# The last attention and the closing rows of a two-block transformer kernel: another order of work, and a value product in two reduced-precision passes

## The chip, the cores and the metric

The kernel runs on one core of a Trainium2 chip. Its inputs and output are fp32 arrays in HBM. The metric is the device time of one execution in microseconds, the median of several. TensorE multiplies matrices into PSUM (eight banks of 128 x 512 fp32), VectorE and ScalarE work on elements, GpSimd does elementwise work in SBUF only, and SyncE issues the DMAs. The engines run their own lists of instructions in order and meet at semaphores.

## The reference

512 tokens of width 1024 go through a first block (sparse attention, pooling, gated FFN) and a second block of two layers: differential attention with a state-space scan, then a sliding-window attention. The change is in that last layer and what follows it:

```python
def sliding_window_attention(q, k, v, sinks, slopes):        # 16 heads of 64, 2 key/value groups, window 128
    ...
    logits = jnp.einsum('bnqkgd,bnskd->bnkgqs', qb, kk).astype(jnp.float32) * scale
    logits = logits - sl * dist.astype(jnp.float32)          # slope of head h: 2 ** (-(h + 1) / 2)
    logits = jnp.where(valid[None, :, None, None], logits, -jnp.inf)
    p = jax.nn.softmax(jnp.concatenate([logits, sink], axis=-1), axis=-1)[..., :-1]
    out = jnp.einsum('bnkgqs,bnskd->bnqkgd', p.astype(v.dtype), vv)
def odd_layer(h, w_in, b_in, sinks, w_out):
    q, k, v, g = jnp.split(h @ w_in + b_in, ODD_SPLITS, axis=-1)
    o = sliding_window_attention(q, k, v, sinks, alibi_slopes(SW_HEADS))
    return (o * jax.nn.silu(g)) @ w_out
x = x + odd_layer(rmsnorm(x, norm_c[j]), ...);  return rmsnorm(x, final_norm)
```

## The kernel before, in words

Activations stand transposed in SBUF: `xt` is the residual, eight tiles `k` of 128 features by 512 tokens. Dense products run in three passes of the reduced fp32 form (`fp32r`): a weight is split into a high part `whi` (ScalarE, `split_hi`) and the rest `wlo` (VectorE, `split_lo`), an activation likewise (`hh`/`hl`, or `ah`/`al`), and `passes` (L290) adds high x high, high x low and low x high. A tile of 128 outputs is 8 x 3 matmuls of 512 columns (`tile_of`, L296). Weights come as items of 256 columns in two slots (`load_item`, L256): SyncE issues an item's two DMAs when the item two before it has been split, TensorE waits for the split (`item_ready`), and each split of a following item waits until TensorE has done with its slot. The lists of all engines are written out by hand; `tiles` counts finished output tiles and `drained` their evictions from PSUM.

The end of the program, in order: `project(..., parts=(0,))` makes the queries of heads 0 to 7; `window_kv` (L2780) the keys and values, with the keys copied to both halves of the partitions and split (`kdh3`, `kdl3`), the values in plain fp32 with zeros beside them (`vp3`); `project(..., parts=(1,))` the other queries, four tiles; then `window_attention` (L2840). It takes 16 heads. On TensorE the slot of head h is: `turn(h-1)` transposes the seven 128 x 128 blocks of probabilities of the head before into banks 4 and 5; `scores(h+1)` computes the four query blocks of the next head into banks 0 to 3, for each two key passes (`kdh3`, `kdl3`) and two passes of distance times a diagonal of the slope (`dg3`, high part and rest); `gate_part(h)` is half a tile of the gate projection into bank 7, work that has nothing to do with the head; `values(h-1)` multiplies the turned probabilities `pt3` in fp32 into bank 6, an even and an odd head added into the two halves of its rows. ScalarE makes the diagonals (L2933), the exponentials (L2960), the high part of the queries, half of the eviction of the turned blocks (L2975), and evicts gate tiles (L2969) and head pairs (L2946). VectorE takes the maxima (L3001 to L3006), scales the probabilities (L3013 to L3017), evicts the other half (L3021) and splits the queries (L2989).

After the last head Silu of the gates, product and splits follow (L3032 to L3046). The residual product with `w_out_c_2` adds into `xt` (`residual`, `last=True`). `final_norm` (L3055) squares the eight tiles (L3063), adds the squares (L3101), multiplies `xt` by the weight on GpSimd (L3072), sums over features on TensorE (L3080), transposes (L3089), scales the rows (L3109) and stores them.

Of the kernel before, what the change touches and what calls it, by code (L numbers as in the profile page):

```python
# [21 lines left out]
P = 128  # L22
S = 512
# [169 lines left out]
def two_blocks(nc, x, par, con, bvc, w, out):  # L193
# [171 lines left out]
    def half_tile(pe, b, t, out, rhs, h, kts=KT, k0=0, first=True, last=True, ready=None):  # L365

        p, cs, ts = b % 2, slice(P * t, P * t + P), token_half(h)
        for k in range(kts):
            if ready:
                pe.wait_ge(ready[0], ready[1] + k + 1)  # L370
            mm = passes(pe, out[:, ts], (whi[:, p, k, cs], wlo[:, p, k, cs]),
# [1190 lines left out]
    def residual(mat, rhs, r0=0, last=False, ready=None):  # L1562
# [21 lines left out]
        @block.scalar  # L1584
        def _(act):
            if last:
                split_hi(act, n0 + 2)
                split_hi(act, n0 + 3)
                return
            with act.Fori(0, 2) as i:  # L1590
                for j in range(2):
                    split_hi(act, n0 + 2 + j, i)

        @block.vector
        def _(dve):
# [8 lines left out]
            if last:  # L1604
                part(0)
                part(1)
                return
# [460 lines left out]
    def diff_attention(m1):  # L2068
# [280 lines left out]
    dt_v, dt_a, cs_done, cs_t, cs_tok, cl_mm, cl_exp = (  # L2349
        sem("dt_v"), sem("dt_a"), sem("cs_done"), sem("cs_t"), sem("cs_tok"), sem("cl_mm"),  # L2350
        sem("cl_exp"))
    x_t, x_tok, st_w, st_mm, st_done, cb_mm, cb_done, s3_pad = (
        sem("x_t"), sem("x_tok"), sem("st_w"), sem("st_mm"), sem("st_done"), sem("cb_mm"), sem("cb_done"),
        sem("s3_pad"))
# [6 lines left out]
    def ssd_inputs():  # L2361
# [29 lines left out]
        def _(act):  # L2391
# [28 lines left out]
            act.wait_ge(dt_v, 1)  # L2420
# [6 lines left out]
        def _(dve):  # L2427
# [16 lines left out]
            dve.wait_ge(drained, m0 + 13)  # L2444
            dve.sem_inc(dt_v, 1)
# [26 lines left out]
    def ssd_core(m1):  # L2472
# [129 lines left out]
        def _(pool):  # L2602
            pool.wait_ge(y_free_for_pad[0], y_free_for_pad[1])
            pool.memset(xpad[:, :, :, :, :], 0.0).then_inc(s3_pad, 1)
            pool.wait_ge(s3_pad, 1)
# [105 lines left out]
    def ssd_norm():  # L2711
# [49 lines left out]
    vp3 = at("vp3", Y + 52 * K, [TT, 320])  # L2761
    pt3 = at("pt3", Y + 58 * K, [2, 7 * P])
# [13 lines left out]
    k3_done, kd3_mm, kd3_done, v3_pad, c4_ready, ns_done = (  # L2776
        sem(n_) for n_ in ("k3_done", "kd3_mm", "kd3_done", "v3_pad", "c4_ready", "ns_done"))
    dg3_done, t3_act, t3_dve, o3_out = (sem(n_) for n_ in ("dg3_done", "t3_act", "t3_dve", "o3_out"))

    def window_kv():  # L2780
# [3 lines left out]
        def _(sp):  # L2784
            load_item(sp, n0, 0, full_item(n0, w["w_in_c_2"], 0, OFF_KV_C))
            sp.wait_ge(z_low, KT)
            sp.dma_start(bv3[:, :], bvc.to_broadcast([P, P])).then_inc(got_con, 16)
# [3 lines left out]

        @block.gpsimd
        def _(pool):
            pool.wait_ge(z_low, KT)
            pool.memset(vp3[:, :, :], 0.0).then_inc(v3_pad, 1)

        @block.tensor
        def _(pe):
# [7 lines left out]
            pe.wait_ge(k3_done, 1)  # L2806
# [4 lines left out]
        def _(act):  # L2811
            split_hi(act, n0 + 2)
            act.wait_ge(got_con, CON4)
            act.activation(dist3[:, :], dist3f[:, :], ACT.Copy).then_inc(c4_ready, 1)
            for g in range(2):
# [345 lines left out]
```

## Time and profile before

| | us |
|---|---|
| median of 3 runs | 1840.81 (1839.79 to 1842.37) |
| the profiled execution, its own time | 1845.26 |
| its span in the trace | 1843.5 |
| TensorE busy in the span | 1673.8 (91%) |
| VectorE, ScalarE, GpSimd busy | 1060.7 (58%), 823.3 (45%), 93.4 (5%) |
| TensorE's granted clock, mean | 0.957 |

In the trace a matmul's record overlaps that of the next, since TensorE is pipelined; starts show the pace. "PEclk" is the granted clock: 1.00 is 2.4 GHz, 0.50 is 1.2 GHz. An engine's idle time matters where another waits for it.

### The profile page before, as it was taken

Reading aid. Unit: us, or ns where it says so; the run is one execution under the profiler, and the core shown is the slowest. Engines: PE = TensorE matmul, PEld = TensorE weight load, DVE = VectorE, ACT = ScalarE, POOL = GpSimd, SP = SyncE. Lnnn points to the kernel's source line nnn. Section 1 sums busy time; section 2 is a strip of 40 time slices with the busy share of each in tenths; the row PEclk is TensorE's granted clock in tenths of the full one; section 3 lists DMA queues with packets and bytes.
Section 4 is the critical chain, followed back from the end, with each engine's and each line's share of the span. In section 5 each row is a group of like instructions: output and inputs, shape, how many; then the busy total and the mean of one; then the engine's idle time right before and its main releaser. Section 6 shows DMA issues by size and latency. Waiting matters only on the chain.

```text
span 1843.5 us, 24067 instructions
## 1 busy us (share of the span) xinstructions
PE 1673.8 (91%) x8860; PEld 1412.3 (77%) x8860; DVE 1060.7 (58%) x1760; ACT 823.3 (45%) x1544; POOL 93.4 (5%) x112
## 2 busy tenths in 40 slices
PE   7998999998999999989999998889987979979977
PEld 6886787886778888868798896668765758859965
DVE  5557877674545656552254438864465984446654
ACT  5545665663334455541132226652353542235641
POOL 2000400000000000000000001100000100000001
PEclk9998999999999999999999999988997989989988
DMA  6411122113431333322223320111320111320011
GB/s 184 125 50 30 46 63 64 46 52 110 141 120 47 101 104 91 91 92 67 99 74 99 108 81 25 35 46 41 102 84 21 47 46 47 99 69 24 28 42 46
DMA packets 147870, 132.95 MB, mean 72 GB/s; under 512 B 8560, under 2 KB 142448, under 8 KB 147776
## 3 DMA queue, kind: packets, MB, share of 16 engines
q1 hardware_dynamic: 143744, 119.58, 21.3%
q0 software_dynamic: 3136, 10.78, 1.6%
q10 hardware_dynamic: 896, 1.32, 0.3%
q8 instruction: 60, 0.98, 0.2%
q14 instruction: 34, 0.28, 0.0%
HBM read 124.33 MB, written 7.34 MB: 71 GB/s over the span
## 4 chain that ended last, share of the span: by engine, by line
PE 74%; DVE 15%; ACT 5%; issue 5%; DMA 1%; DVEq 0%; ACTq 0%; POOL 0%
PE bank L292 19%; PE bank L293 19%; PE bank L294 19%; DVE wlo L285 2%; PE bank L1206 2%; PE bank L1220 2%; ACT whi L278 1%; PE bank L1189 1%; PE bank L2911 1%; DVE ptl L1374 1%; DVE sz L2700 1%; PE bank L2870 1%; PE bank L1223 1%; PE bank L2278 1%; PE bank L2883 1%
## 5 line engine op out<-in xcount | busy, mean ns | idle before, releaser
L292 PE MATMUL bank<-hh,whi 128*128 128x512 f32 (+3 forms) x1208 | 466.2, 386 | 16.0 <-DVE wlo L285 5.6
L293 PE MATMUL bank<-hl,whi 128*128 128x512 f32 (+3 forms) x1208 | 455.7, 377 | 0.0
L294 PE MATMUL bank<-hh,wlo 128*128 128x512 f32 (+3 forms) x1208 | 455.2, 377 | 0.0
L278 ACT ACTIVATE whi<-wraw 128x2048 fp32r<-128x2048 f32 x111 | 212.1, 1913 | 338.6 <-PE bank L294 338.5
L285 DVE TENSOR_TENSOR wlo<-wraw,whi 128x2048 fp32r<-128x2048 f32 x111 | 254.1, 2289 | 178.7 <-ACT whi L278 177.3
L292 PEld LDWEIGHTS bank<-hh,whi 128*128 128x128 f32 (+2 forms) x1208 | 231.2, 191 | 60.9 <-issue 5.8
L294 PEld LDWEIGHTS bank<-hh,wlo 128*128 128x128 f32 (+2 forms) x1208 | 230.5, 191 | 43.3
L293 PEld LDWEIGHTS bank<-hl,whi 128*128 128x128 f32 (+2 forms) x1208 | 231.2, 191 | 39.1 <-issue 0.7
L1374 DVE TENSOR_TENSOR ptl<-bank,pth 128x128 fp32r<-128x128 f32 (+3 forms) x128 | 56.8, 485 | 64.4 <-ACT pth L1282 63.0
L292 PE MATMUL bank<-ah,whi 128*128 128x512 f32 (+1 forms) x224 | 83.8, 374 | 10.6 <-DVE al L3046 8.3
L292 PE MATMUL bank<-yh,whi 128*128 128x512 f32 (+1 forms) x220 | 79.3, 360 | 6.7 <-DVE yl L1740 6.7
L1264 ACT ACTIVATE pr<-bank,nm 128x128 f32<-128x128 f32 (+3 forms) x128 | 66.7, 531 | 39.8 <-DVE nm L1357 39.8
L293 PE MATMUL bank<-al,whi 128*128 128x512 f32 (+1 forms) x224 | 82.1, 367 | 0.0
L294 PE MATMUL bank<-ah,wlo 128*128 128x512 f32 (+1 forms) x224 | 81.9, 366 | 0.0
L293 PE MATMUL bank<-yl,whi 128*128 128x512 f32 (+1 forms) x220 | 76.8, 349 | 0.0
L294 PE MATMUL bank<-yh,wlo 128*128 128x512 f32 (+1 forms) x220 | 76.7, 349 | 0.0
L1282 ACT ACTIVATE pth<-bank 128x128 fp32r<-128x128 f32 (+3 forms) x128 | 49.0, 438 | 50.4 <-PE bank L1206 50.1
L1206 PE MATMUL bank<-ident,pr 128*128 128x128 f32 x320 | 47.5, 279 | 14.9 <-DVE ptl L1374 10.9
L1206 PEld LDWEIGHTS bank<-ident,pr 128*128 128x128 f32 x320 | 33.8, 141 | 34.5 <-issue 31.9
L292 PEld LDWEIGHTS bank<-ah,whi 128*128 128x128 f32 x224 | 43.2, 193 | 21.0 <-issue 9.4
L2007 POOL TENSOR_TENSOR kl<-k,kh 64x512 fp32r<-64x512 f32 x16 | 22.2, 1388 | 673.2 <-ACT kh L1984 672.7
L292 PE MATMUL bank<-whi,hh 128*128 128x256 f32 (+1 forms) x192 | 54.5, 284 | 1.1 <-DVE k L1924 1.1
(393 smaller groups left out, 3212.2 us busy)
## 6 DMA issues: line engine op xcount, KB each, us to landing
wraw<-in_w_in_a_dram SPq DMA_DIRECT2D x52, 512.0 KB, 4.5
wraw<-in_w_up_dram SPq DMA_DIRECT2D x42, 512.0 KB, 4.9
wraw<-in_w_in_dram SPq DMA_DIRECT2D x34, 512.0 KB, 4.8
wraw<-in_w_in_c_dram SPq DMA_DIRECT2D x18, 512.0 KB, 4.7
wraw<-in_w_down_dram SPq DMA_DIRECT2D x16, 512.0 KB, 4.0
wraw<-in_w_out_a_dram SPq DMA_DIRECT2D x16, 512.0 KB, 4.0
aside<-stage POOLq DMA_DIRECT2D x20, 256.0 KB, 2.3
wraw<-in_w_attn_br_dram SPq DMA_DIRECT2D x8, 512.0 KB, 4.0
```

The costliest lines, as they stand in the source:

```text
L278: act.activation(whi[:, p], wraw[:, p], ACT.Copy).then_inc(w_hi_done, 1)
L285: dve.tensor_tensor(wlo[:, p], wraw[:, p], whi[:, p].bitcast(F32), ALU.subtract).then_inc(w_lo_done, 1)
L292: pe.matmul(out, ws[0], hs[0], start=first, stop=False)
L293: pe.matmul(out, ws[0], hs[1], start=False, stop=False)
L294: return pe.matmul(out, ws[1], hs[0], start=False, stop=last)
L1189: pe.matmul(bank[i][:, 0:wd], qs[:, p % 2, e, P * i:P * i + P], part[:, b, p // 4, 0:wd], start=(part is kdh), stop=False)
L1206: mm = pe.transpose(bank[4 + (n > 0)][:, c0 + P * j:c0 + P * j + P], pr[:, u % 2, POFF[i] + P * j:POFF[i] + P * j + P], ident[:, :])
L1220: mm = pe.matmul(out[:, P * j:S], vhl[:, j, b, g, :], part[:, j, P * j:S], start=(b == 0 and j == 0 and part is pth), stop=False, skip_gro ...
L1264: act.activation(pr[:, u % 2, POFF[i]:POFF[i] + wd], bank[i][:, 0:wd], ACT.Exp, bias=nm[:, u % 2, i:i + 1], accum_out=sm[:, u % 2, i:i + 1 ...
L1282: ins = act.activation(pth[to], src, ACT.Copy)
L1374: ins = dve.tensor_tensor(ptl[to], src, pth[to].bitcast(F32), ALU.subtract)
L2007: ins = pool.tensor_tensor(kl2[rows, h % 2, m, :], k2[rows, h, :], kh2[rows, h % 2, m, :].bitcast(F32), ALU.subtract)
```

## The change

- Attention: the four tiles of later queries move into `window_attention`, between the first scores and the loop, into banks 6, 7, 4 and 5. The diagonals are made by GpSimd; where a slope's high part is the slope itself (odd h), its second pass is left out.
- Values: kept as high and low part side by side (`vhl3`, 64 + 64 columns). Turned probabilities are split into `pth3` (ScalarE) and `ptl3` (VectorE). A product of the two passes has, in bank 6, the sum for the high value part in rows 0 to 63 and that for the low part in rows 64 to 127; ScalarE copies the lower half out (`out_half`), VectorE adds the upper (`out_sum`), once per head.
- The Silu, gated products and splits are interleaved with the last head.
- `final_rows` takes the place of the last `residual` and of `final_norm`: each finished tile of the residual is transposed at once, squared with a sum per row on ScalarE, multiplied by a row of weights (`wrow`, fetched by its own DMA from the longer `bvc` input) on VectorE; the last two tiles are computed in token halves, and the rows are scaled in place.
- Small ones: `half_tile` gets an offset `w0`; some semaphores are replaced by others in the scan, with the same order.

```diff
@@ window_kv
-            for tt in range(TT):
-                ...
-            ins.then_inc(drained, 1)
+            dve.tensor_tensor(v3[:, :, :], bank[1][:, :].rearrange("p (t d) -> p t d", t=TT),
+                              bv3[:, :].unsqueeze(1).to_broadcast([P, TT, P]), ALU.add).then_inc(drained, 1)
+            for g in range(2):
+                dve.wait_ge(v3_high, g + 1)
+                dve.tensor_tensor(vhl3[:, :, g, HD:P], v3[:, :, HD * g:HD * g + HD], vhl3[:, :, g, 0:HD].bitcast(F32),
+                                  ALU.subtract).then_inc(v3_low, 1)
@@ window_attention, TensorE
-                    pe.matmul(out, dg3[:, h % 2, 1, :], dist3[:, lo:2 * P], start=False, stop=True).then_inc(s_done, 1)
+                    if not exact(h):
+                        mm = pe.matmul(out, dg3[:, h % 2, 1, :], dist3[:, lo:2 * P], start=False, stop=True)
+                    mm.then_inc(s_done, 1)
@@ values
-                    mm = pe.matmul(bank[6][:, P * j:P * j + n], vp3[:, j, c0:c0 + P],
-                                   pt3[:, h % 2, 2 * P * j:2 * P * j + n], start=(e == 0 and j == 0),
-                                   stop=(e == 1 and j == TT - 1), skip_group_check=True)
+                pe.wait_ge(t3_dve, 2 * h + 2)
+                if h:
+                    pe.wait_ge(o3_out, h)
+                    for p in (pth3, ptl3):
+                        mm = pe.matmul(bank[6][:, P * j:P * j + n], vhl3[:, j, g, :],
+                                       p[:, h % 2, 2 * P * j:2 * P * j + n], start=(j == 0 and p is pth3),
+                                       stop=(j == TT - 1 and p is ptl3), skip_group_check=True)
@@ TensorE's list
+            pe.wait_ge(drained, d0)
+            query_tile(0)
+            query_tile(1)
+            pe.wait_ge(c4_ready, 1)
+            pe.wait_ge(kd_low, 10)
+            pe.wait_ge(v3_low, 2)
             scores(0)
+            query_tile(2)
+            scores(1)
+            query_tile(3)
+            gate_part(0)
+            for h in range(1, NH + 1):
+                turn(h - 1)
+                if h + 1 < NH:
+                    scores(h + 1)
+                if h < NH:
+                    gate_part(h)
+                values(h - 1)
@@ ScalarE's list
+            for h in range(1, NH):
+                if h >= 2:
+                    expo(h)
+                if h % 2 == 0:
+                    gate_out(h // 2 - 1)
+                high(h - 1)
+                if h >= 2:
+                    out_half(h - 2)
+                if h % 2 and h // 2 + 2 < NH // 2:
+                    queries_high(h // 2 + 2)
+                if h % 4 == 0:
+                    split_hi(act, n0 + h // 4 + 1)
+            for k in range(4):
+                silu(k)
+            high(NH - 1)
+            out_half(NH - 2)
+            gate_out(KT - 1)
+            for k in range(4, KT):
+                silu(k)
+                gated_high(k - 4)
+            out_half(NH - 1)
+            ...
@@ VectorE's list
+            for h in range(1, NH):
+                if h >= 2:
+                    maxima(h)
+                    scaled(h - 1)
+                if h % 2 == 0 and h // 2 + 1 < NH // 2:
+                    queries_low(h // 2 + 1)
+                if h % 4 == 1 and h > 1:
+                    split_lo(dve, n0 + h // 4 + 1)
+                low(h - 1)
+                if h >= 2:
+                    out_sum(h - 2)
+            scaled(NH - 1)
+            gated_prod(0)
+            gated_prod(1)
+            low(NH - 1)
+            out_sum(NH - 2)
+            ...
+            split_lo(dve, n0 + 5)
@@ GpSimd
+                if h >= 2:
+                    pool.wait_ge(s_done, SD3 + 4 * (h - 1))
+                ins = pool.tensor_scalar(dg3[:, h % 2, 0, :], ident[:, :], hi_, 1.0, ALU.mult, ALU.mult)
@@ final_rows, SyncE
+            with sp.Fori(0, 2) as i:
+                for j in range(2):
+                    load_item(sp, n0 + j, i, full_item(n0 + j, mat, 0, IC * j + 2 * IC * i))
+            sp.wait_ge(tiles, 2 * n0)
+            sp.dma_start(wrow[:, :], bvc[:, P:P + D].to_broadcast([P, D])).then_inc(got_con, 16)
+            for t, ends in ((0, 1), (1, 1), (2, 2), (3, 2)):
+                sp.wait_ge(y_fin if t % 2 == 0 else x_w, ends)
+                sp.dma_start(out[P * t:P * t + P, :], orow[:, t, :]).then_inc(stored, 16)
@@ TensorE (turn(n) transposes block n of xt once drained says that its tile is added)
+            for k in range(6):
+                ...
+                tile_of(pe, n0 + k // 2, k % 2, bank[k % 4][:, :], rhs, ready=ready if k == 0 else None) \
+                    .then_inc(tiles, 1)
+                if k:
+                    turn(k - 1)
+            ...
+            half_tile(pe, n0 + 3, 1, bank[1], rhs, 1, last=False, kts=4)
+            turn(8)
+            half_tile(pe, n0 + 3, 1, bank[1], rhs, 1, first=False, kts=4, k0=4, w0=4).then_inc(tiles, 1)
+            turn(9)
@@ ScalarE
+                for t in range(t0, t1):
+                    ins = act.activation(sqj[:, n % 4, P * t:P * t + P], bank[4 + n % 4][:, P * t:P * t + P], ACT.Square,
+                                         accum_out=ssq[:, t, k:k + 1])
+            ...
+            root(0)
+            squares(8)
+            scaled_row(1)
+            squares(9)
+            root(1)
+            scaled_row(3)
@@ VectorE
+            dve.wait_ge(got_con, CON4 + 16)
+            for k in range(6):
+                add(k)
+                ...
+            half_add(6, 1)
+            row(7)
+            inverse(0)
+            scaled_row(0)
+            row(8)
+            half_add(7, 1)
+            row(9)
+            inverse(1)
+            scaled_row(2)
```

## Rows read from the trace of the kernel before

**Rows 1.** Stretches: us long; busy PE, PEld, DVE, ACT, POOL; PEclk, DMA share, GB/s.

```profile
1616.80:1641.30 24.50, 23.50 (x96) 19.12 (x96) 6.76 (x12) 1.92 (x1) 0.00 (x0) 0.93 0.27 86
1641.30:1647.35 6.05, 0.16 (x2) 0.04 (x1) 4.41 (x4) 5.25 (x8) 0.00 (x0) 0.82 0.04 7
1647.35:1669.47 22.12, 18.77 (x89) 17.17 (x90) 9.15 (x27) 9.17 (x35) 0.00 (x0) 0.74 0.14 46
1669.47:1759.25 89.78, 89.78 (x561) 81.35 (x560) 59.36 (x158) 55.74 (x181) 0.00 (x0) 1.00 0.11 36
...
1767.70:1783.17 15.47, 7.00 (x19) 5.17 (x19) 10.80 (x16) 11.70 (x18) 0.00 (x0) 0.67 0.20 68
1783.17:1823.07 39.90, 39.83 (x174) 32.50 (x174) 10.13 (x11) 4.88 (x5) 0.00 (x0) 1.00 0.00 0
1823.07:1843.50 20.43, 6.77 (x40) 6.53 (x40) 13.66 (x18) 5.32 (x8) 8.10 (x8) 0.74 0.25 103
```

**Rows 2.** Timeline of TensorE, one head: start us, us, instruction.

```profile
1717.65 0.93 PE L2883 MATMUL bank<-ident,pr 128*128 128x128 f32 x7
1718.33 0.30 PE L2870 MATMUL bank<-kdh,qs 128*128 128x128 f32 x1
...
1720.30 0.40 PE L292 MATMUL bank<-hh,whi 128*128 128x512 f32 x1
...
1723.04 1.68 PE L2911 MATMUL bank<-pt,vp 128*128 128x256 f32 x8
1724.56 0.49 PE L2883 MATMUL bank<-ident,pr 128*128 128x128 f32 x3
```

**Rows 3.** Timeline of VectorE, one head.

```profile
1712.95 1.38 DVE L2989 TENSOR_TENSOR qs<-q,qs 64x512 fp32r<-64x512 f32 x2 [0.55 <-ACT qs L2941]
1714.26 0.28 DVE L3001 TENSOR_REDUCE nm<-bank 128x1 f32<-128x128 f32 x1
...
1715.50 0.23 DVE L3006 TENSOR_SCALAR nm<-nm,nsink 128x4 f32<-128x4 f32 x1
...
1716.04 1.07 DVE L3017 TENSOR_SCALAR pr<-pr,rs 128x128 f32<-128x128 f32 x4
...
1719.22 2.28 DVE L285 TENSOR_TENSOR wlo<-wraw,whi 128x2048 fp32r<-128x2048 f32 x1
1721.42 0.28 DVE L3001 TENSOR_REDUCE nm<-bank 128x1 f32<-128x128 f32 x1
```

**Rows 4.** Groups by form, whole span: xcount | busy us, mean ns | idle before, releaser.

```profile
L1374 DVE TENSOR_TENSOR ptl<-bank,pth 128x512 fp32r<-128x512 f32 x32 | 22.0, 688 | 3.8 <-ACT pth L1282 2.3
...
L1282 ACT ACTIVATE pth<-bank 128x512 fp32r<-128x512 f32 x32 | 19.1, 597 | 2.9 <-PE bank L1206 2.9
```

**Rows 5.** Timeline of ScalarE, same head.

```profile
1715.77 0.37 ACT L2960 ACTIVATE pr<-bank,nm 128x128 f32<-128x128 f32 x1 [0.51 <-DVE nm L3006]
...
1717.47 0.30 ACT L2964 ACTIVATE es<-nm,parm 128x4 f32<-128x4 f32 x1
```

**Rows 6.** Groups of GpSimd, 1590 to 1844 us.

```profile
L3072 POOL TENSOR_SCALAR xw<-xt,parm 128x512 f32<-128x512 f32 x8 | 8.1, 1029 | 297.6 <-PE bank L294 297.6
```

**Rows 7.** Groups by form of VectorE, 1760 to 1843 us.

```profile
L3101 DVE TENSOR_TENSOR ssn<-ssn,sqn 128x512 f32<-128x512 f32 x7 | 6.9, 990 | 0.7
...
L3043 DVE TENSOR_TENSOR q<-q,sg 128x512 f32<-128x512 f32 x8 | 5.4, 686 | 1.1 <-ACT sg L3032 1.1
```

**Rows 8.** Timeline of ScalarE at the first Silu.

```profile
1767.73 0.60 ACT L2946 ACTIVATE q<-bank 128x512 f32<-128x512 f32 x1 [0.78 <-PE bank L2911]
1768.35 1.28 ACT L3032 ACT_TABLE_LOAD   x1
1769.64 0.72 ACT L3032 ACTIVATE sg<-sg,parm 128x512 f32<-128x512 f32 x1
```

**Rows 9.** DMA issues, 1510 to 1600 us: KB each, us to landing.

```profile
bv<-in_bvc_dram SPq DMA_DIRECT2D x1, 64.0 KB, 4.6
```

**Rows 10.** Timeline of SyncE, the output's DMAs.

```profile
1836.29 4.48 SPq L3116 DMA_DIRECT2D out_dram<-orow  x4
```

More of the change, by code:

```diff
@@ L363, in token_half, with half_tile @@
         return slice(HS * h, HS * h + HS)
-    def half_tile(pe, b, t, out, rhs, h, kts=KT, k0=0, first=True, last=True, ready=None):
+    def half_tile(pe, b, t, out, rhs, h, kts=KT, k0=0, w0=0, first=True, last=True, ready=None):
         p, cs, ts = b % 2, slice(P * t, P * t + P), token_half(h)
@@ L1560, in block1_merge, with residual @@
         return (g_low, AHEAD)
-    def residual(mat, rhs, r0=0, last=False, ready=None):
+    def residual(mat, rhs, r0=0, ready=None):
         n0, m0 = new_items(4), new_tiles(KT)
@@ L1602, in part @@
                         split_lo(dve, n0 + 2 + t // 2, i)
[L1604 to L1607, printed above, removed]
             with dve.Fori(0, 2) as i:
@@ new lines, in scaled @@
+            def scaled(v):
+                dve.wait_ge(p_exp, SD3 + 5 * v + 5)
+                if v:
+                    dve.wait_ge(p_scaled, D3 + 4 * v)
+                dch(dve, dve.tensor_tensor(sm3[:, v % 2, :], sm3[:, v % 2, :], es3[:, v % 2, :], ALU.add))
+                dch(dve, dve.reciprocal(rs3[:, v % 2, :], sm3[:, v % 2, :]))
+                for i in range(TT):
+                    part = pr3[:, v % 2, i, (P if i == 0 else 0):2 * P]
+                    dve.tensor_scalar(part, part, rs3[:, v % 2, i:i + 1], None, ALU.mult).then_inc(p_scaled, 1)
@@ new lines, in root, with scaled_row @@
+            def root(h):
+                act.wait_ge(n_sum, c["sum"] + h + 1)
+                act.activation(rtn[:, 2 * h:2 * h + 2], ssr[:, 2 * h:2 * h + 2], ACT.Sqrt, bias=eps[:, 1:2],
+                               scale=1.0 / D).then_inc(n_inv, 1)
+            def scaled_row(t):
+                act.wait_ge(n_inv, c["inv"] + t + 1)
+                act.activation(orow[:, t, :], orow[:, t, :], ACT.Copy, scale=rrn[:, t:t + 1]).then_inc(x_w, 1)
+            split_hi(act, n0 + 2)
+            for n in range(8):
+                squares(n)
+                if n == 1:
+                    split_hi(act, n0 + 3)
@@ L3119, in two_blocks @@
+            half_add(6, 0)
+            row(5)
+            half_add(7, 0)
+            row(6)
+            half_add(6, 1)
[7 more added lines that the diff above has]
+            scaled_row(2)
     stored = sem("stored")
@@ L3136, in two_blocks @@
     window_kv()
-    m1 = project(w["w_in_c_2"], 0, q3, SCALE, bias="b_q", parts=(1,)) + KT
-    ready = window_attention(m1)
-    mx = residual(w["w_out_c_2"], (ah, al), ready=ready, last=True)
-    final_norm(mx)
+    ready = window_attention()
+    final_rows(w["w_out_c_2"], (ah, al), ready)
     assert count["item"] == TOTAL_ITEMS, count
```

420 lines of the change are left out of this document (224 added, 196 removed).

## The prediction

> **What bounds the kernel now.** Read first the table of stretches [rows 1]: it cuts the last 227 us at the points where TensorE's work changes kind. In the long row 1669.47 to 1759.25, the attention's steady part, TensorE is busy all 89.78 us at the full 2.4 GHz level; VectorE is busy 59, ScalarE 56. Thirteen heads fit in it (turn(1) to turn(14)), so a head takes 6.91 us, and TensorE's order sets it. Around it TensorE waits: 6 us before the first scores (1641.30 to 1647.35), a filling of two heads at a mean clock of 0.74, 15.5 us of gating (1767.70 to 1783.17, 19 matmul records), and 20.43 us of closing norm, where it has 40. The diff touches these stretches and hardly anything ahead of 1616.8, so I leave the first 1616.8 us as they are.
>
> Then the timeline of one head [rows 2]: turn at 1717.65, scores from 1718.33 (16 matmuls in 1.97 us, 0.123 each), gate part from 1720.30 (12 in 2.74 us, so a whole 24-matmul tile is 5.48), values from 1723.04 in eight records, next turn at 1724.56: 1.52 us for the values.
>
> **Attention, one head on TensorE.** The value product becomes 8 matmuls (four row groups, a high and a low pass) of the reduced fp32 form. This stage has no such product; the nearest row is the scores' spacing of 0.123. Seven of the eight spacings count fully and the last 128-column pair less, so I take 0.90. Ends: 0.8, and 1.52 if each were as slow as a record of today. That removes 0.62. For the eight odd heads the second slope matmul goes: 4 x 0.12 = 0.47. A head is then 0.70 + 1.92 + 2.74 + 0.90 = 6.26, or 5.79 with an odd head's scores. From turn(1) to turn(14) there are 13: 7 x 5.79 + 6 x 6.26 = 78.1.
>
> **Who is late next.** VectorE for one head: maxima to the end of the scaling 2.85 (1714.26 to 1716.04 + 1.07) [rows 3]; the new low part of the turned probabilities reads 384 and 512 columns from PSUM; the same form of block 1 takes 0.69 for 512 [rows 4], I take 0.55 for 384, and starts come some 0.08 closer than these, so 1.08; the new sum of the two row groups 0.60, taken like the 512-column form less overlap; the query split 1.30 every second head and the weight split 2.20 (1719.22 to 1721.42) every fourth [rows 3]. Mean: 2.85 + 1.08 + 0.60 + 0.65 + 0.55 = 5.73, against 6.03 for TensorE. ScalarE: exponentials 1.9 (1715.77 to 1717.47 + 0.22 [rows 5]), two high parts 0.91 and a half of the output 0.50 [rows 4], about 1.3 of eviction, queries and weights: 4.6. None alone is the bound, but they are chained. After maxima(h) (1.4) come the exponentials (1.95), on even heads a gate eviction (0.51), the two high parts (0.9), the second low part (0.65) and the sum (0.6): about 6.2 from maxima to maxima, 5.7 on odd heads. With a weight split ahead of the low part, VectorE's list is 2.85 + 2.20 + 1.08 + 0.60 = 6.73. So the next scaling comes 0.36 to 0.43 us late twice in four heads. I add 6 x 0.4 = 2.4: turn(1) to turn(14) takes 80.5, 6.19 a head, instead of 89.78. Ends: 78.1 with nothing late, and 89.8 if the chain costs all that TensorE saves. **Gain 9.3.**
>
> The slope diagonals move to GpSimd: at most two 128-column products a head. No row shows such a product at 128 columns; the xw rows take 1.03 for 512 columns [rows 6], so 0.26 each, asked for two heads ahead. In the closing norm VectorE's two-SBUF add takes 0.990 beside them, while the same form takes 0.686 with GpSimd idle [rows 7], so 0.30 is lost per 1.03 of GpSimd, at most 0.15 a head. A diagonal is released by the end of the scores two heads back, just when VectorE starts the PSUM maxima of that head; I take nothing, and 0.15 x 14 = 2.1 as the end. The Trainium skill (GPSIMD Engine Reference, Specifications) says that the two engines contend where VectorE runs a 2-port mode or has two SBUF inputs; by it the maxima, low parts and sums would not be slowed and only the two kinds of split would, which the slowed add agrees with.
>
> **Front of the attention.** TensorE starts again near 1617.8 in both: the values' bias add is still behind the weight split. Before, four projection tiles, the wait and two filling heads end at turn(1), 1669.47. After: two tiles 10.96, plus 1.6 for the cold start (today's row has 24.5 for four tiles, 21.9 at full spacing, 1.0 of it ahead of the first), to 1630.4; scores(0) 1.9; tile 5.5; scores(1) 1.45; tile 5.5, to 1644.7. The whole softmax of heads 0 and 1 lies beside these tiles. gate_part(0) waits for the last query eviction: 0.9. Then 2.74, and turn(0), scores(2), gate(1), values(0) at 6.26: turn(1) at 1654.6. **Gain 14.9.** If the first two softmaxes weren't hidden, their latency of about 5 us a head would come back; the order of the list leaves 12 us for them.
>
> **End of the attention to the end of the first closing tile.** Before: turn(14) at 1759.25; the last seven tiles of 5.48 end at 1823.07, so the first ends at 1784.7, 25.5 us later. After: turn(14), gate(15), values(14) 4.36; turn(15) 0.70; ScalarE's list puts the table load (1.28 [rows 8]) and four Silu ahead of high(15), so values(15) waits 3.0, then 0.9 and 0.9 more until the first low part of the gated product; the products and splits run on VectorE at 1.21 per k (two of 0.60), with the last sum between, and four k's follow closely: 8.3. Sum 18.2; plus 1.3 because TensorE is at half rate for part of it, as in today's gating (0.67 [rows 1]). 1735.1 + 19.5 = 1754.6. **Gain 6.0.**
>
> The Trainium skill (ScalarE: Activation LUTs, What ACT_TABLE_LOAD costs) gives a switch 1283 ns and a drain of about 1380 more. Here the load follows an activation that ends at 1768.33 and the Silu starts at 1769.64 [rows 8], so the drain isn't in the trace; by the page the two loads on the new path would cost some 2.8 us more, which I leave out.
>
> **Closing tiles.** Five whole tiles 27.4, 96 half-width matmuls at 0.12 = 11.5, and 30 transposes put between at the turn's spacing of about 0.11 = 3.3, against 38.4. One new wait: VectorE's first residual add waits for the final weight row. On SP's queue its DMA stands behind the fourth weight item, which waits for the split that VectorE does last in the attention (end about 1754.6 in the new times), then two issues (0.9), then itself: the small broadcast of this region landed 4.6 after issue [rows 9], and this one is 512 KB behind 1 MB. So add(0) ends near 1761.4, and turn(0), due at 1758.7 + 1.3, stands about 2.7 with all of TensorE behind it. Ends: 0 (landed earlier) and 6. Last matmul 1754.6 + 42.2 + 2.7 = 1799.5. **Loss 6.5** against 38.4.
>
> **Tail.** Before, 20.43 from 1823.07: eight squares and adds chained at some 1.0 each [rows 7], then sums, root, 32 transposes, rows out. After, following the last matmul: the half add (held 1.1 by a row scaling on VectorE) 1.5, two transposes 0.4, two squares 0.8, row 0.4, sum, root and reciprocal 0.8, scaling 1024 columns 1.0: 4.9. The output: today the fourth issue ends at 1840.77 and the span at 1843.5 [rows 10], 2.7 later, or 3.1 with the issue itself; two 512 KB rows now leave together, so 1.2 more. 9.2 in all, **gain 11.2**; I take a table load of 1.28 for the root as hidden but for what the half add shows.
>
> **Sum.** 14.9 + 9.3 + 6.0 - 6.5 + 11.2 = 34.9 us. The profiled execution took 1845.26 with 1843.5 in the span; it becomes 1810.4. Runs without the profiler have their median 4.45 below, 1840.81: forecast **1806** (1.9% faster).
>
> **Rivals.** (a) The attention becomes bound by the VectorE and ScalarE chain more than I count: VectorE's list is at 95% of TensorE's, and each 0.1 us on every crossing of engines adds it several times. At 6.6 us a head, 13 x 0.4 = 5 us later: 1811. For it: busy shares near each other; against: 0.05 us from maxima to exponential in [rows 3, 5]. Chance 0.22. (b) The two-pass value product doesn't do what it says, its passes costing as much as today's records: 0.62 x 16 = 10 back, 1816. Against: the scores, which are matmuls of the same form, at 0.123. Chance 0.06. (c) The weight row lands in time and the closing stretch is smoother: 3 to 6 less, 1801. For it: the 4.6 of [rows 9] stands behind 1 MB of weights too. Chance 0.17. (d) The other side: the gaps before each turn keep the granted clock at the lower level through the attention. Heads then cost what the matmul spacing does at 1.2 GHz, about 1.9 times 6.03 = 11.5, so 14 x 5.3 = 74 more: 1880, slower. It decides from 35 / 14 = 2.5 us more a head. For it: the clock was 0.74 while the pipeline filled; against: it was 1.00 through 90 busy us, and my gaps are 0.4. Chance 0.02. (e) The forecast as it stands: 0.53.
>
> **How the numbers follow.** The ends of the value product, the contention, the weight row and the chain reach from 1796 (all good) to 1817 (rival b with some of a); I give 1797 to 1816. A change under 0.2%, 3.7 us, couldn't be told from none. Every case but (d) is faster by 20 us or more: faster 0.97, same 0.01, slower 0.02.
>
> **What would show it.** Turn to turn (line of the transposes) 5.8 and 6.3 us alternating, with short waits on the scaled probabilities; values in 0.9; TensorE without a gap over 1 us from 1617 to the last head; one stall of some 3 us after the second closing tile, ended by the first residual add; about 9 us from the last closing matmul to the end. The prediction is wrong if a head takes over 6.6 us, if the clock row shows less than 1.00 in the attention, or if the tail is above 13.

## The result, and the profile after

The changed kernel takes 1810.05 us (median of 4 runs, 1808.80 to 1811.56) against 1840.30 of the kernel before in the same session: ratio 0.9834, 95% interval 0.9817 to 0.9851. Forecast 1806, range 1797 to 1816. The profiled execution took 1809.91, its span is 1808.1.

First the page of the changed kernel: busy time by engine.

```profile
PE 1650.0 (91%) x8868; PEld 1390.5 (77%) x8868; DVE 1072.5 (59%) x1792; ACT 836.4 (46%) x1597; POOL 94.2 (5%) x127
```

TensorE is busy 23.8 us less (1673.8 before). Of that 5.7 lies ahead of the changed part, in the same 7844 matmuls (1480.5 before, 1474.8 now), so it isn't the change's. In the changed part it is busy 193.4 before and 175.2 now, 18.2 less; the other 14.6 of the 32.8 us that this part became shorter is waiting that went. Where, the table of stretches of the changed kernel shows. It is cut at the same events as [rows 1], except that the fourth row ends, and the fifth begins, where the second closing tile starts (1784.76 before): restart of TensorE behind the key and value tiles, turn(1), turn(14), second closing tile, last closing matmul's end, end. Columns as in [rows 1].

```profile
1615.19:1651.93 36.74, 35.80 (x179) 30.27 (x180) 21.72 (x43) 17.80 (x43) 3.43 (x5) 0.96 0.27 86
1651.93:1733.48 81.55, 79.88 (x533) 72.46 (x532) 72.22 (x183) 60.07 (x174) 4.80 (x16) 1.00 0.12 40
1733.48:1752.41 18.93, 15.01 (x66) 12.28 (x67) 16.42 (x30) 17.42 (x29) 0.00 (x0) 0.82 0.00 1
1752.41:1799.84 47.43, 44.03 (x247) 38.20 (x245) 16.65 (x23) 14.13 (x65) 0.00 (x0) 0.96 0.10 34
1799.84:1808.10 8.26, 0.49 (x3) 0.20 (x2) 2.31 (x7) 2.87 (x7) 0.00 (x0) 0.65 0.64 254
```

| stretch, us | before | forecast | after | gain forecast | gain measured |
|---|---|---|---|---|---|
| restart to turn(1) | 51.67 | 36.8 | 36.74 | 14.9 | 14.9 |
| turn(1) to turn(14) | 89.78 | 80.5 | 81.55 | 9.3 | 8.2 |
| turn(14) to second closing tile | 25.51 | 19.5 | 18.93 | 6.0 | 6.6 |
| to the end of the last closing matmul | 38.31 | 44.9 | 47.43 | -6.5 | -9.1 |
| to the end | 20.43 | 9.2 | 8.26 | 11.2 | 12.2 |
| sum | 225.70 | 190.9 | 192.91 | 34.9 | 32.8 |

The cuts of [rows 1] at turn(1) and turn(14) lie 0.16 behind the first transpose of each (1669.31 and 1759.09); those of the later tables lie at it. Cut alike, the first three rows of before are 51.51, 89.78 and 25.67, the gains 14.8, 8.2 and 6.7.

The timeline of TensorE, one head of the changed kernel (the answer to [rows 2]): the last value products and the next turn.

```profile
1700.41 0.39 PE L294 MATMUL bank<-hh,wlo 128*128 128x512 f32 x1
1700.63 0.28 PE L2915 MATMUL bank<-pth,vhl 128*128 128x256 f32 x1
...
1701.39 0.27 PE L2915 MATMUL bank<-ptl,vhl 128*128 128x128 f32 x1
1702.07 0.98 PE L2889 MATMUL bank<-ident,pr 128*128 128x128 f32 x7 [0.41 <-DVE pr L3061]
```

The eight passes start 0.11 to 0.12 apart. Where the next turn doesn't wait, it starts 0.87 after the first of them; in six of the thirteen heads it starts 0.1 to 0.3 later than that, in three 0.57. Starts of the turns lie 6.3 (even scores) and 5.9 (odd) apart, except where a weight split stands in VectorE's list: 6.88, then 6.16. The bracket is the wait of that head: VectorE scaled the probabilities 0.41 too late.

ScalarE's and TensorE's timelines between the last turns and the gating, changed kernel (the answer to [rows 8]):

```profile
1735.13 0.59 ACT L2983 ACTIVATE osum<-bank 64x512 f32<-64x512 f32 x1
1735.74 1.28 ACT L2987 ACT_TABLE_LOAD   x1
1737.04 1.95 ACT L2987 ACTIVATE sg<-sg,parm 128x512 f32<-128x512 f32 x3
...
1742.11 0.55 PE L2915 MATMUL bank<-pth,vhl 128*128 128x256 f32 x1 [2.96 <-DVE q L3074]
```

The load starts 0.02 behind the end of the copy before it and the Silu 0.02 behind the load: no idle time beside the load's 1.28 is seen.

The closing tiles, changed kernel, timelines of SyncE, VectorE and TensorE. The weight row's DMA is issued behind the fourth weight item, VectorE's first residual add waits for it, TensorE's first transpose for the add.

```profile
1753.93 0.93 SPq L263 DMA_DIRECT2D wraw<-in_w_out_c_dram  x2
1755.07 0.35 SPq L3149 DMA_DIRECT2D wrow<-in_bvc_dram  x1
...
1757.63 0.39 PE L294 MATMUL bank<-ah,wlo 128*128 128x512 f32 x1
...
1760.67 1.28 DVE L3232 TENSOR_TENSOR xt<-xt,bank 128x512 f32<-128x512 f32 x2 [6.98 <-DMA wrow<-in_bvc_dram]
1761.42 1.12 PE L3168 MATMUL bank<-ident,xt 128*128 128x128 f32 x4 [3.40 <-DVE xt L3232]
1762.18 0.78 PE L292 MATMUL bank<-ah,whi 128*128 128x512 f32 x1
```

Behind the 3.40 us the matmuls start 0.43 apart instead of 0.227: from 1761.42 to 1764.70 the granted clock is 0.50, 1.2 GHz.

The tail of the changed kernel, by timeline (the answer to the last row of [rows 1] and to [rows 10]):

```profile
1800.11 4.47 SPq L3152 DMA_DIRECT2D out_dram<-orow  x4
1800.33 0.41 DVE L3240 TENSOR_TENSOR xt<-xt,bank 128x256 f32<-128x256 f32 x1
1800.79 0.44 PE L3168 MATMUL bank<-ident,xt 128*128 128x128 f32 x2 [0.90 <-DVE xt L3240]
1801.93 0.42 DVE L3247 TENSOR_TENSOR orow<-bank,wrow 128x256 f32<-128x256 f32 x1 [1.19 <-ACT sqj L3203]
1802.99 1.15 ACT L3214 ACTIVATE orow<-orow,rrn 128x1024 f32<-128x1024 f32 x1 [0.23 <-DVE rrn L3255]
```

### The profile page after: what moved, and what is told of

Read it like the earlier page. It is cut to its first block, busy times and chain, and to the rows that moved or that the text cites. A ratio compares the mean times of both kernels' runs of the same rounds, so it can differ in the third digit from the quotient of the medians.

```text
span 1808.1 us, 24172 instructions
## 1 busy us (share of the span) xinstructions
PE 1650.0 (91%) x8868; PEld 1390.5 (77%) x8868; DVE 1072.5 (59%) x1792; ACT 836.4 (46%) x1597; POOL 94.2 (5%) x127
## 4 chain that ended last, share of the span: by engine, by line
PE 69%; DVE 17%; ACT 6%; issue 6%; DMA 1%; POOL 0%; ACTq 0%; DVEq 0%; SPq 0%
PE bank L292 19%; PE bank L294 18%; PE bank L293 18%; DVE wlo L285 2%; PE bank L1206 2%; PE bank L1220 2%; ACT whi L278 2%; PE bank L1189 1%; DVE ptl L1374 1%; DVE sz L2688 1%; PE bank L1223 1%; DVE kl L1991 1%; DMA gs<-aside 1%; PE bank L2270 1%; ACT pr L2960 1%
## 5 line engine op out<-in xcount | busy, mean ns | idle before, releaser
L1206 PE MATMUL bank<-ident,pr 128*128 128x128 f32 x320 | 47.5, 279 | 14.9 <-DVE ptl L1374 11.0
L292 PEld LDWEIGHTS bank<-yh,whi 128*128 128x128 f32 x220 | 42.2, 192 | 17.4 <-DVE yl L1732 7.2
```

What stands on the lines that cost most here:

```text
L292: pe.matmul(out, ws[0], hs[0], start=first, stop=False)
L1206: mm = pe.transpose(bank[4 + (n > 0)][:, c0 + P * j:c0 + P * j + P], pr[:, u % 2, POFF[i] + P * j:POFF[i] + P * j + P], ident[:, :])
```

## The experiments

"The stretch" below is always that from TensorE's restart to the end, 192.91 in the changed kernel; it leaves out the unchanged part ahead. Medians are of 5 or more runs, that of the fp32 values of 4. The first four ran beside each other (kernel before: 1842.16), the next four (1840.98) and the last four (1842.32) likewise.

**The changed kernel once more.**

> The changed kernel unaltered, on the chip of this call, as the mark for the others. My theory of the 4 us by which the forecast was low: the one profiled execution of the kernel before was 4.5 to 5 us above its own median, 2.4 us of that lying ahead of the changed part, so the gain read from two traces (35) is more than the gain of the medians (30). By it the ratio of medians stays at 0.9834 within 0.002 (30 us) and the part of the trace from the restart of TensorE behind the key and value tiles to the end repeats within 0.5 us (192.9 us). Rival: the first medians were off by chance; then this call shows 34 to 35 us, ratio 0.981.

1810.21 us, ratio 0.9830 (0.9816 to 0.9843). The median is as expected, and turn(1) to turn(14) is 81.54. The stretch isn't: 191.6, 1.4 less than the 192.9 that was to repeat within 0.5. All of it, and a little more, lies between the second closing tile and the end of the last closing matmul, 45.84 for 47.43:

```profile
1748.95:1794.79 45.84, 42.47 (x247) 36.92 (x245) 16.67 (x23) 14.13 (x65) 0.00 (x0) 1.00 0.10 35
```

```profile
1757.92 0.66 PE L3168 MATMUL bank<-ident,xt 128*128 128x128 f32 x4 [3.37 <-DVE xt L3232]
1758.34 0.48 PE L292 MATMUL bank<-ah,whi 128*128 128x512 f32 x1
1758.65 0.39 PE L293 MATMUL bank<-al,whi 128*128 128x512 f32 x1
```

The same kernel has the same wait (3.37, 3.40), but behind it the granted clock stays at 1.00 here and fell to 0.50 in the first trace. This run is the comparison for the next three.

**The weight row's DMA ahead of the fourth weight item.**

```diff
-            with sp.Fori(0, 2) as i:
-                for j in range(2):
-                    load_item(sp, n0 + j, i, ...)
-            sp.wait_ge(tiles, 2 * n0)
-            sp.dma_start(wrow[:, :], ...)
+            for b in range(4):
+                if b == 3:
+                    sp.wait_ge(s_done, SD3 + 4 * NH)
+                    sp.dma_start(wrow[:, :], ...)
+                load_item(sp, n0 + b, 0, ...)
```

> The weight row's DMA is issued ahead of the fourth closing weight item, as soon as the last scores are done. Theory: the wait of 3.4 us before the first closing transposes is this DMA's alone, and the half-rate stretch behind it (transposes 1.12 instead of 0.44, six matmuls at 0.43 instead of 0.23) another 1.8, so 5 us go: ratio to before near 0.981. Rival 1: the wait only moves to the next tile's split or add, and 1 us or less is won. Rival 2: the clock stays low for want of the earlier work's pace and only the 3.4 go.

1806.76 us, ratio 0.9812 (0.9799 to 0.9826), 3.5 less than the changed kernel beside it. The row was issued at 1729.91. Table of stretches of this kernel, turn(14) to the end:

```profile
1733.64:1752.61 18.97, 15.22 (x67) 12.39 (x68) 16.46 (x30) 17.42 (x29) 0.00 (x0) 0.82 0.00 1
1752.61:1794.86 42.25, 42.25 (x247) 36.99 (x245) 16.71 (x23) 14.18 (x65) 0.00 (x0) 1.00 0.08 26
1794.86:1803.10 8.24, 0.48 (x3) 0.20 (x2) 2.32 (x7) 2.87 (x7) 0.00 (x0) 0.78 0.64 255
```

The closing tiles take 42.25, all busy and at 1.00: the forecast for them without the wait was 42.2. So the wait cost 47.43 - 42.25 = 5.2 us in the first trace of the changed kernel, 3.40 of standing and some 1.8 of slow matmuls behind it, and 45.84 - 42.25 = 3.6 in its repeat, where the clock didn't fall. The other six kernels here that have this wait (3.25 to 4.05 us) take 47.5 to 49.3 for the same stretch, so the slow matmuls behind it are the common case and the repeat is the exception. The medians give 3.5, from runs that spread over 7 to 9 us, and so can't choose between the two.

**The weight splits of the attention's loop, three, on GpSimd.**

```diff
@@ GpSimd, in the loop over the diagonals
+                if h in (7, 11, 15):
+                    split_lo(pool, n0 + (h - 2) // 4 + 1)
@@ VectorE
-                if h % 4 == 1 and h > 1:
-                    split_lo(dve, n0 + h // 4 + 1)
...
+            dve.wait_ge(w_lo_done, n0 + 5)
             split_lo(dve, n0 + 5)
```

> The three weight splits of heads 5, 9 and 13 move from VectorE to GpSimd. Theory: they are what makes the next scaling late; turn to turn goes from 6.88 and 6.16 to 6.3 and 5.85 at those heads, 1.0 us each time, 2.9 in all. Rival: GpSimd's split (about 5 us, two inputs in SBUF) slows VectorE's query split and the scaling beside it, as the closing adds were slowed from 0.69 to 0.99, and less than 1 us or nothing is won.

1824.65 us, ratio 0.9912 (0.9897 to 0.9927), 14.4 slower than the changed kernel. The timelines of GpSimd and VectorE of this run:

```profile
1667.58 4.53 POOL L285 TENSOR_TENSOR wlo<-wraw,whi 128x2048 fp32r<-128x2048 f32 x1 [1.48 <-ACT whi L278]
1667.60 4.54 DVE L3052 TENSOR_SCALAR nm<-nm,nsink 128x4 f32<-128x4 f32 x1
```

VectorE's 128x4 operation, else 0.23, started 0.02 behind GpSimd's split and ended with it. TensorE then stood 4.24 us for the scaled probabilities, three times, and the slot behind each stand took 7.9, the first at a granted clock of 0.79. Turn(1) to turn(14) took 96.38. The rival had the direction right; it named other operations, the query split and the scaling.

**Values in one fp32 pass without the zeros.** The product as 64 columns of plain fp32, nothing to split or to add, the new order kept.

```diff
-                    for p in (pth3, ptl3):
-                        mm = pe.matmul(bank[6][:, P * j:P * j + n], vhl3[:, j, g, :], p[...], ...)
+                    mm = pe.matmul(bank[6][0:HD, P * j:P * j + n], v3[:, j, HD * g:HD * g + HD], pt3[...], ...)
```

> The two-pass value product alone undone inside the new order: one fp32 product per head of 64 columns, the turned probabilities only copied (half by ScalarE, half by VectorE), the sum of row groups gone. Theory: TensorE sets the pace; a value product takes 1.5 instead of 0.87 us, and heads come at 6.44 (odd scores) and 6.9 without the 0.26 us of mean stall: 13 heads take 86.7 instead of 81.6, the kernel is 5 to 6 us slower than the changed one. Rival: VectorE and ScalarE set it, and the lighter lists make the kernel no slower or faster (within 1 us).

1818.62 us, ratio 0.9876 (0.9861 to 0.9891), 8.4 slower. TensorE's timeline of this run, values and turn:

```profile
1684.22 1.73 PE L2914 MATMUL bank<-pt,v 128*64 128x256 f32 x8
1685.88 0.98 PE L2888 MATMUL bank<-ident,pr 128*128 128x128 f32 x7
```

1.66 us for the values against 0.87, slots of 7.20 and 6.72, turn(1) to turn(14) 90.24 with TensorE busy all of it, though VectorE has 12.6 less to do there (59.65 for 72.22). TensorE's work sets the pace, as the theory had it; the extra was larger, because the product took 1.66 where the theory had 1.5.

**Last high part ahead of two Silu.**

```diff
-            for k in range(4):
-                silu(k)
+            silu(0)
+            silu(1)
             high(NH - 1)
             out_half(NH - 2)
+            silu(2)
+            silu(3)
```

> ScalarE takes the high part of the last head's probabilities and the copy of head 14 after two Silu of the gates instead of after four; the other two Silu follow. In the changed kernel's trace TensorE stands 2.96 us before the last value product. Theory: that wait costs little by itself, because VectorE's chain (products, low parts, sums, splits) sets when the first closing tile can run; two Silu less (0.6 each) ahead of it give 0.7 to 0.9 us in the trace from turn(14) to the last closing matmul, and no difference to be told in the medians. Rival: the 2.96 us before the last value product are the price, so nearly all of them go, 2.5 to 3 us, and the median falls from 1810 to 1807.

1809.51 us, ratio 0.9818 (0.9796 to 0.9840): no difference to be told. TensorE and VectorE of this run:

```profile
1744.31 0.36 PE L2915 MATMUL bank<-pth,vhl 128*128 128x256 f32 x1 [2.15 <-DVE q L3076]
1746.43 0.69 DVE L3085 TENSOR_TENSOR al<-q,ah 128x512 fp32r<-128x512 f32 x1 [1.05 <-ACT ah L2991]
1747.27 0.77 PE L292 MATMUL bank<-ah,whi 128*128 128x512 f32 x1 [1.85 <-DVE al L3085]
```

The wait before the values falls from 2.96 to 2.15, and a new one of 1.85 stands ahead of the first closing matmul. The bracket on `al` says whose: ScalarE's high part, which has the same Silu ahead of it in either order. Turn(14) to the last closing matmul's start: 66.56, before 66.13. The 0.7 to 0.9 us of the theory didn't come, nor the 2.5 to 3 of the rival; only that the medians wouldn't tell was right. The chain starts at ScalarE, not at VectorE.

**The new closing rows alone, on the kernel before.**

> The kernel before with the new closing rows alone (and the scan's semaphores): attention, gates and value product are those of before. Theory, by the changed kernel's trace: the stretch from the last closing matmul to the end falls from 20.9 to 8.5 us, the closing tiles with transposes between them take 3.8 longer, and the wait for the weight row is small, since the fourth weight item is split before the attention has ended; gain 7.5 to 9 us, 1832 to 1833.5. Rival: the weight row is late here too (3 us and a half-rate stretch behind it); gain 3 to 5, 1836 to 1837.5.

1831.70 us, ratio 0.9946 (0.9925 to 0.9967). Stretches, cut as above:

```profile
1613.82:1665.17 51.35, 42.03 (x183) 35.90 (x184) 19.32 (x38) 16.32 (x44) 0.00 (x0) 0.84 0.20 62
1665.17:1754.96 89.79, 89.79 (x562) 81.36 (x560) 59.34 (x158) 55.69 (x181) 0.00 (x0) 1.00 0.11 36
1754.96:1780.63 25.67, 16.27 (x69) 12.80 (x68) 14.91 (x25) 15.58 (x23) 0.00 (x0) 0.80 0.17 61
1780.63:1822.91 42.28, 42.28 (x247) 37.00 (x245) 15.56 (x22) 14.03 (x65) 0.00 (x0) 1.00 0.00 1
1822.91:1831.20 8.29, 0.48 (x3) 0.20 (x2) 2.31 (x7) 2.86 (x7) 0.00 (x0) 0.64 0.63 253
```

Attention and gating are those of before; the row, issued at 1766.53, is there when the first tile is done. The median fell by 9.3, the stretch by 8.3, as the theory had it.

**The new attention alone, with the old closing.**

> The changed kernel's attention with the residual product and final norm of the kernel before. Theory: the front gives 14.9, turn(1) to turn(14) 8.2 and the gating some 5 us, so the gain is 27 to 29 us, 1812.5 to 1815; with the closing alone the two sum to 3 to 5 us more than the whole change gives, which is the wait for the weight row, since only the two together have it. Rival: the attention's gains are partly lost when TensorE meets the next chain earlier (the clock falls in the gating and the old norm takes longer at the lower level); gain 22 to 25, and the parts sum to the whole or to less.

1813.12 us, 27.9 less than before, ratio 0.9849 (0.9824 to 0.9873): the theory. The first three stretches are 37.05, 81.55 and 18.91, as in the changed kernel; the other two, as in the kernel before:

```profile
1752.59:1790.67 38.08, 38.08 (x169) 31.34 (x167) 10.61 (x10) 4.87 (x4) 0.00 (x0) 1.00 0.08 28
1790.67:1811.30 20.63, 6.89 (x41) 6.49 (x40) 13.70 (x18) 5.32 (x8) 8.10 (x8) 0.74 0.26 103
```

Stretches: 217.38 with the closing alone (8.3 less than 225.7), 196.22 with the attention alone (29.5 less), 192.91 with both (32.8 less). The parts sum to 37.8, 5.0 more than the whole (3.6 more than its repeat, 191.6): the weight row's wait, which only the whole has. Its first closing tile is done at 1752.4, and the row is issued at 1755.1; with the closing alone these are 1780.6 and 1766.5.

**The row's DMA, the Silu order, and the last half add ahead of the first row scaling.**

> The changed kernel with three edits: the weight row's DMA ahead of the fourth weight item, the last high part ahead of two of the Silu, and in the closing the last half add ahead of the first row scaling on VectorE. Theory: 3.4 us (measured in the run with the row moved) + 0.8 + 0.8 = 4.5 to 5.5 us faster than the changed kernel, 1804.5 to 1806. Rival: the two small edits only move a wait (the row scaling then ends the chain instead of the half add, and VectorE sets the gating in either order), so it equals the run with the row alone moved, 1806.8.

1806.21 us, ratio 0.9803 (0.9781 to 0.9824). Stretch 187.96, with the row alone moved 188.05: the rival. The half add came 0.4 sooner behind the last matmul, but the first row scaling 0.9 later, and the first output DMA with it; the tail became 0.1 shorter. The Silu order made turn(14) to the second closing tile 0.3 longer, as it did alone.

**The weight splits in halves, one in each odd head.**

```diff
-                if h % 4 == 1 and h > 1:
-                    split_lo(dve, n0 + h // 4 + 1)
+                if h % 2 and h > 4:
+                    split_lo_half(dve, n0 + h // 4 + 1, h % 4 // 2)     # 128 x 1024 of wlo each
```

> The changed kernel with VectorE's three weight splits inside the attention loop (2.28 us each) cut into two halves of 1.15, one each in the slots of the odd heads 5 and 7, 9 and 11, 13 and 15, where VectorE stands idle 1.29 us. Theory: those splits are what makes the slots 6.88 (wait of 0.4 for the scaled probabilities) and the next 6.16; without them all odd slots take 5.8 to 5.9 and all even ones 6.3, so turn(1) to turn(14) falls from 81.55 to 79.0 to 79.5, 2 to 2.5 us. Rival: the chain over ScalarE is as long without the splits, the waits come back spread over the heads, and the stretch stays above 81.

1809.56 us, ratio 0.9827 (0.9803 to 0.9851); the median tells nothing, the trace does. VectorE's half split, and the stretch from turn(1) to turn(14) in the same trace:

```profile
1671.62 1.22 DVE L290 TENSOR_TENSOR wlo<-wraw,whi 128x1024 fp32r<-128x1024 f32 x1
1653.76:1732.97 79.21, 79.21 (x533) 72.34 (x532) 71.69 (x186) 60.16 (x174) 4.80 (x16) 1.00 0.08 28
```

79.21 for 81.55, TensorE busy all of it, no slot above 6.4. By the starts of the values and of the next turn, 0.87 apart where nothing waits, thirteen heads waited 2.9 us in the changed kernel and 0.65 here. So the three splits made all but some 0.1 in each odd slot. The stretch to the end is 192.1 even so: the front took 1.6 longer in this trace, at a lower clock (last section).

**The second slope pass kept in the odd heads.** `exact(h)` returns False, so the odd heads get a product with a diagonal of zeros.

> The changed kernel with the second slope pass kept for every head: four matmuls and one GpSimd diagonal more in each odd head. Theory: 4 x 0.12 = 0.47 a head where TensorE sets the pace (six odd heads in turn(1) to turn(14)), partly swallowed where it stood waiting 0.4 (three of them): 2 to 2.8 us more in that stretch, 81.55 to 83.6 to 84.3, and 0.5 to 1 us more around it; median 1812.5 to 1813.5. Rival: VectorE's and ScalarE's chain sets the pace of the loop, TensorE's extra matmuls are hidden in its waits, under 1 us more.

1813.41 us, ratio 0.9837 (0.9818 to 0.9856). Turn(1) to turn(14), slots of 6.3 and of 6.50 where a split stands:

```profile
1658.94:1741.38 82.44, 82.28 (x561) 75.51 (x561) 72.22 (x183) 60.32 (x174) 6.48 (x22) 1.00 0.12 40
```

Only 0.9 more, the rival's number and not the theory's 2 to 2.8. The rival's reason doesn't hold: the 28 extra matmuls take 28 x 0.118 = 3.3 us, TensorE is busy all but 0.16, and a plain odd slot takes 6.29 where it took 5.81 with nothing waiting. With the halves the stretch was 79.21; 79.2 + 3.3 comes near this run's 82.4. So each pass costs its full price, and the extra work took the place of nearly all the waiting that the splits had made, more than the theory let it swallow. The median of 1813.41, inside the expected range, is luck. Dropping the pass, one of the change's own steps, was worth 0.9 us in this stretch for want of the halves.

**All four edits: row, Silu order, half add, halves.**

> The changed kernel with the weight row's DMA earlier, the last high part ahead of two Silu, the last half add first, and the weight splits in halves. Theory: 5 us (weight row, measured) and 2 to 2.5 (splits) add up, since they lie in different stretches: 1802.5 to 1804 against 1810. Rival: a faster attention meets the closing weights' items earlier than they are there, so the halves' gain comes back as a wait in the closing tiles, and it equals the version without halves, 1806.

1803.86 us, ratio 0.9799 (0.9778 to 0.9820). Stretch 185.69 against 187.96 without the halves and 192.91 in the changed kernel, 191.6 in its repeat: the halves' 2.3 come on top of the row's gain, as the theory had it. The fastest version here, 38 us below the kernel before.

**The GpSimd split in eight pieces.** As the third experiment, each split as eight instructions of 256 columns.

> The run with the four weight splits on GpSimd, each cut into eight instructions of 256 columns (0.57 us each by 4.53 / 8). In the uncut run VectorE's 128x4 operation, started beside GpSimd's, lasted 4.54 us instead of 0.23. Theory: VectorE's operation is held only until GpSimd's present instruction ends, so cut up it waits 0.6 at most and the loop from turn(1) to turn(14), 96.4 us uncut, falls to 82 to 86; 1811 to 1815. Rival: GpSimd keeps the shared access until its row of instructions is through, or holds each of VectorE's SBUF operations in turn, and the loop stays above 90.

1816.87 us (three splits, as in the third experiment), ratio 0.9853 (0.9834 to 0.9872). Turn(1) to turn(14) 89.72, above the theory's 82 to 86 and just under the rival's 90. TensorE stood 2.03 us three times, and the slot behind took 7.9, the granted clock at 0.78 in it. GpSimd by groups, and VectorE beside it:

```profile
L291 POOL TENSOR_TENSOR wlo<-wraw,whi 128x256 fp32r<-128x256 f32 x24 | 17.1, 746 | 4.4 <-ACT whi L278 4.4
```

```profile
1671.24 0.75 DVE L3059 TENSOR_SCALAR nm<-nm,nsink 128x4 f32<-128x4 f32 x1
1671.91 0.15 DVE L3066 TENSOR_TENSOR sm<-sm,es 128x4 f32<-128x4 f32 x1
1672.09 0.18 DVE L3067 RECIPROCAL rs<-sm 128x4 f32<-128x4 f32 x1
1672.30 2.65 DVE L3070 TENSOR_SCALAR pr<-pr,rs 128x128 f32<-128x128 f32 x4
```

The 128x4 operation is held 0.5, one piece, as the theory had it; but so is each of the four scalings (2.65 for 1.07), as the rival had it. Both are right in part: the hold lasts one instruction and comes with every such operation.

## Why the prediction was right, and where its terms were off

- **Front, 14.9: measured 14.9, 14.8 cut alike.** No softmax latency came back (one wait of 0.94, forecast 0.9), so the mechanism is right. The last 0.1 is luck: the front of the same code took 36.7 to 38.3 over these traces. No run has the new order of the query tiles alone; the run without the new closing shows the front's gain with the rest of the attention's changes. The unchanged part ahead wasn't equal: the restart was at 1617.8 before and 1615.19 after, and lay between 1611.5 and 1621.4 over these traces.
- **Heads, 9.3: 8.2.** Values 0.87 (forecast 0.90). The stalls came where VectorE's list has a weight split, and cost 81.55 - 79.21 = 2.3 by the run with halves (forecast 6 x 0.4 = 2.4). The 0.36 to 0.43 for each was near (0.41 in the trace), though its working isn't shown, and the terms of the chain add to 6.0 where the text says 6.2. The missing 1.1 is in the plain slots: 5.9 for 5.79 in the odd ones, 6.31 for 6.26 in the even ones. Some 0.65 of it is small waits, by the run with halves. Rival (a), that the chain costs 0.4 more in every head, was false: without the splits it costs 0.05. Rival (b) was false too; the new order with an fp32 pass instead is 8.4 slower.
- **Diagonals on GpSimd, nothing: right.** They take 0.30 each (estimate 0.26), and VectorE's groups are unchanged (maxima of 512 columns 0.68, query split 0.69, weight split 2.28). But the prediction's list of what GpSimd would slow, only the two kinds of split, was wrong: what the runs with the split on GpSimd show held are the `TENSOR_SCALAR` behind the maxima and those of the scaling.
- **Gating, 6.0: 6.6, 6.7 cut alike.** TensorE's wait of 2.96 was forecast at 3.0. The chain is ScalarE's (Silu order), and the clock there was 0.82.
- **Closing tiles, -6.5: -9.1. The mis-sized term** is the weight row's wait, forecast at 2.7 and measured at 5.2 in the first trace, 3.6 in the repeat; the tiles and transposes were right (42.25 with the row early, forecast 42.2). The mechanism was as written. The 2.7 isn't what the prediction's own times give: with turn(0) due at 1758.7 + 1.3 and the add's end near 1761.4, the wait is 1.4. It was 3.40, because the split that the fourth item waits for ended 1.3 behind the first closing tile's end (1753.69, 1752.41), where the prediction had both at 1754.6, and because the row landed 7.0 behind that split's end, where the prediction had some 6.1. And the sum had nothing for the lower clock behind the wait, 1.8 more in one trace and 0.2 in the other. Rival (c), the row in time, was false here; the run with the DMA moved makes it true.
- **Tail, 11.2: 12.2.** From the last matmul's end to the last row scaling 3.2 (1799.84 to 1802.99), where the forecast had 3.9, and from there 5.1, where it had 5.3. In that 5.3 the 1.2 for two rows that leave together had no row behind it; only the sum of the last part can be compared.
- **From trace to median.** The sum gave 34.9 where the trace gives 32.8; from the median of 1840.81 that makes 1808.0, and 1810.05 was measured. The medians differ by 30.3, and by 31.9 in the next session, the spans by 35.4, of which 2.6 is the later restart. The repeat's trace would give 34.1. So 1 to 2.5 us between trace and medians stay unexplained; the median of the kernel before alone moved by 2.0 between sessions (1840.30 to 1842.32).
- **What was to show it** did: slots, values, one stall of about 3 us ended by the first residual add, 8.3 from the last matmul to the end. A gap over 1 us came at the last head (2.96), as counted. The Trainium skill (ScalarE: Activation LUTs, What ACT_TABLE_LOAD costs) has a drain of some 1380 ns with each switch to another table set; the rows of the gating show 0.02 on either side of the load.

## What to carry to other kernels

When a faster stage ends sooner, look at what is queued behind it on the DMA issuer: a small transfer behind a weight item, which itself waits for a late split, cost 3.6 us in one trace and 5.2 in another, of 38 in all, and moving that one DMA gave it back. Count a wait of TensorE of some us at its length at least: the matmuls behind it may run at the lower clock, as they did behind this wait in seven of eight traces. Where TensorE sets a loop's pace and the next engine is at 90% of it, find the heads in which the second engine has an extra item and cut that item in two: the rest of the loop needn't change.

## What the runs showed that was not expected

- A GpSimd instruction with two SBUF inputs holds a VectorE `TENSOR_SCALAR` from SBUF to SBUF for as long as it lasts: 4.54 us for one of 0.23, 0.75 beside pieces of 0.75. TensorE stands 4.24 for it each time; with the slower slot behind, each uncut split on GpSimd costs the loop (96.38 - 79.21) / 3 = 5.7 us. Beside the pieces the low parts from PSUM, the reciprocal (0.18) and the 128x4 add of two SBUF inputs (0.15) kept their times; the query split never ran beside them. The Trainium skill (SBUF — State Buffer, Who interferes with whom) says that the first to start takes the shared pair of ports for its whole instruction and that `tensor_scalar` can be in the mode that needs it; the traces agree, 4.54 beside 4.53. GpSimd's own pieces took 0.746, for 4.53 / 8 = 0.57; why isn't shown.
- An fp32 value product of 64 columns took 1.66 us, no less than that of 128 columns with zeros before (1.52 [rows 2]).
- The same code after the same wait of 3.22 us, at the restart, ran at different clocks: 6 matmuls 0.43 apart in the changed kernel's trace, 14 in that of the halves, 1.6 us more. The first 15 us in the tables of stretches of the two (granted clock 0.91 and 0.80):

```profile
1615.19:1630.40 15.21, 15.21 (x69) 12.77 (x70) 5.67 (x10) 6.66 (x10) 0.67 (x2) 0.91 0.22 69
```

```profile
1615.45:1630.70 15.25, 15.25 (x60) 12.52 (x61) 5.01 (x9) 5.12 (x9) 0.00 (x0) 0.80 0.21 69
```

Such differences move a span by more than an edit of 1 us does. Stretches help only where the clock stays at 1.00 in both: turn(1) to turn(14) repeats within 0.06 over six traces with the same code in it, the closing tiles of the same kernel differ by 1.6.
